# Attention transposed in halves, its sums taken from ones beside V and inverted on GpSimd

## The reference

```python
def one_block(qi):
    s = jnp.einsum('bqhgd,bshd->bhgqs', qi, k).astype(jnp.float32)
    p = jax.nn.softmax(s, axis=-1).astype(v.dtype)
    return jnp.einsum('bhgqs,bshd->bqhgd', p, v)
...
def conformer_conv(u, conv_dw, conv_b, ln_g, ln_b, w_o):
    a, gt = u[..., :CONV_W], u[..., CONV_W:]
    g = a * jax.nn.sigmoid(gt)
```

## Time and profile before

| | |
|---|---|
| median of three runs | 2191.34 us (2189.56 to 2195.04) |
| the profiled execution's own time | 2191.78 us |
| its span, first to last instruction | 2190.0 us |
| PE busy | 2124.9 us, 97% |
| PE weight loads busy | 1789.5 us, 82% |
| DVE busy | 1329.9 us, 61% |
| ACT busy | 804.8 us, 37% |
| GpSimd busy | 787.1 us, 36% |
| mean granted clock of TensorE | 0.986 |

### The profile page before, as it was taken

The page is one execution under the profiler, slowest core; times in us unless marked ns, Lnnn a source line. Parts: engine busy times, 40 slices in busy tenths (PEclk is TensorE's granted clock), DMA queues, the critical chain, the costliest instruction groups (busy, mean ns, idle before and its releaser), DMA issues.

```text
span 2190.0 us, 28107 instructions
## 1 busy us (share of the span) xinstructions
PE 2124.9 (97%) x11340; PEld 1789.5 (82%) x11340; DVE 1329.9 (61%) x1809; ACT 804.8 (37%) x1189; POOL 787.1 (36%) x366
## 2 busy tenths in 40 slices
PE   9999999999999999999999999899999999999997
PEld 7877888888888888888888887778777877888885
DVE  7369899855873688847616785989854362111113
ACT  5457411233224522222212356662244353222223
POOL 3310123232435433323323365004344475444442
PEclk8999999999999999999999999999999999999998
DMA  7100012132453234533323313002232423322321
GB/s 274 58 30 1 25 57 64 34 121 92 142 164 108 73 128 126 183 116 126 106 78 115 93 66 111 20 1 82 86 93 82 143 79 97 96 94 90 96 87 67
DMA packets 63200, 202.62 MB, mean 93 GB/s; under 512 B 7136, under 2 KB 8416, under 8 KB 63072
## 3 DMA queue, kind: packets, MB, share of 16 engines
q1 hardware_dynamic: 58608, 191.56, 27.0%
q10 hardware_dynamic: 4464, 9.28, 1.2%
HBM read 195.17 MB, written 5.64 MB: 92 GB/s over the span
## 4 chain that ended last, share of the span: by engine, by line
PE 80%; DVE 15%; ACT 3%; issue 1%; DMA 1%; POOL 1%; ACTq 0%; DVEq 0%; POOLq 0%
PE ps L560 73%; DVE conv_acc L1716 3%; DVE ps L1716 2%; DVE unit_stats L1677 2%; PE ps L586 1%; DVE pt1l L1697 1%; DVE pt0l L1697 1%; DVE probs L1691 1%; PE ps L795 1%; PE ps L629 1%; PE ps L647 1%; PE ps L638 1%; PE ps L816 1%; PE ps L668 1%; DMA w_raw<-in_w 1%
## 5 line engine op out<-in xcount | busy, mean ns | idle before, releaser
L455 POOL TENSOR_TENSOR w_l<-w_raw,w_h 128x1024 fp32r<-128x1024 f32 (+3 forms) x296 | 677.3, 2293 | 1283.0 <-ACT w_h L954 1282.9
L560 PE MATMUL ps<-h_h,w_h 128*128 128x512 f32 (+1 forms) x1296 | 428.0, 370 | 8.4 <-ACT t L1234 4.2
L560 PE MATMUL ps<-h_l,w_h 128*128 128x512 f32 (+1 forms) x1296 | 425.2, 368 | 0.0
L560 PE MATMUL ps<-h_h,w_l 128*128 128x512 f32 (+1 forms) x1296 | 424.7, 368 | 0.0
L954 ACT ACTIVATE w_h<-w_raw 128x1024 fp32r<-128x1024 f32 (+3 forms) x296 | 277.5, 939 | 236.0 <-PE ps L560 148.7
L560 PEld LDWEIGHTS ps<-h_h,w_h 128*128 128x128 f32 x1296 | 243.3, 188 | 59.0 <-ACT t L1234 6.0
L560 PEld LDWEIGHTS ps<-h_h,w_l 128*128 128x128 f32 x1296 | 244.4, 189 | 44.0
L560 PEld LDWEIGHTS ps<-h_l,w_h 128*128 128x128 f32 x1296 | 243.9, 188 | 42.6 <-issue 1.2
L1547 DVE CUSTOM_DVE_ANT_0 ps<-ada_raw,c_row 128x1024 f32<-128x1024 f32 x160 | 271.0, 1694 | 10.5 <-DMA ada_raw<-in_ada 5.4
L560 PE MATMUL ps<-f_h,w_h 128*128 128x258 f32 (+1 forms) x672 | 173.1, 339 | 0.9 <-DVE t L1902 0.9
L560 PE MATMUL ps<-f_h,w_l 128*128 128x258 f32 (+1 forms) x672 | 173.5, 340 | 0.0
(11 more groups left out here) (256 smaller groups left out, 3220.9 us busy)
## 6 DMA issues: line engine op xcount, KB each, us to landing
w_raw<-in_w SPq DMA_DIRECT2D x216, 512.0 KB, 3.6
ada_raw<-in_ada SPq DMA_DIRECT2D x80, 512.0 KB, 3.7
w_raw<-in_w SPq DMA_DIRECT2D x56, 256.0 KB, 3.2
w_raw<-in_w SPq DMA_DIRECT2D x16, 384.0 KB, 3.1
ada_near<-in_ada SPq DMA_DIRECT2D x10, 512.0 KB, 10.2
ada_far<-in_ada SPq DMA_DIRECT2D x6, 512.0 KB, 14.8
x_again<-in_x ACTq DMA_DIRECT2D x8, 384.0 KB, 7.5
x_between<-x SPq DMA_DIRECT2D x8, 384.0 KB, 2.9
```

The source lines that it names most:

```text
L455: nc.gpsimd.tensor_tensor(wl[:, s % RING, 0:n], raw[:, s % RAW, 0:n], wh[:, s % RING, 0:n], ALU.subtract).then_inc(split, 1)
L560: ins = nc.tensor.matmul(at(out, c0, c1), w[:, s % RING, b * P:(b + 1) * P], m[:, kt, first + c0:first + c1], start=(kt == 0 and n == 0), ...
```

## The change

- The exponential leaves the probabilities as they are: they are no longer summed on ACT nor multiplied on DVE. V's high part is kept once for each key-value head, as 64 columns of V beside 64 columns of ones. The value product with it gives the output on partitions 0 to 63 and, on partitions 64 to 127, the sum of the probabilities, 64 times over. Both are evicted, the sum into `ada_raw` (`o_sum`).
- For each pair of heads GpSimd then runs `divide_by_sums`: `pow(sum, -1)`, three instructions for one Newton step on it, and the multiplication of `o_raw`. Each waits for the one before it.
- Transposes, high parts and low parts come in halves of three (or two) blocks, and each half of B is a buffer of its own.
- The transposes of a unit wait for its exponential alone; the value products start one turn of the loop later.
- The scores of units 0 and 1 are issued inside the gemm of `cval` (after five and seven of its eight blocks), unit 0 into OD; their maxima and the first exponential move ahead in DVE's and ACT's programs.
- `o_high` and `o_low` of the last row block come later: behind the gate of the next convolution block on ACT, behind the first eleven taps on DVE. GpSimd's weight splits after the first of attention wait behind all four divisions.

```diff
+            def divide_by_sums(ly, lo, j):
+                last_b = max(b for h, _, _, _, _, b in units(ly) if h == 2 * j + 1)
+                pool.wait_ge(*seen("free", "pv", ly, last_b))
+                total, inverse = o_sum(j)[:, lo:T], (t1[:, lo:T] if j < BR - 1 else o_sum(j - 1)[:, lo:T])
+                chain(nc.gpsimd.tensor_tensor(inverse, total, minus_one[:, 0:1].to_broadcast([P, T - lo]), ALU.pow))
+                chain(nc.gpsimd.tensor_tensor(total, total, inverse, ALU.mult))
+                chain(nc.gpsimd.tensor_scalar(total, total, -1.0, 2.0, ALU.mult, ALU.add))
+                chain(nc.gpsimd.tensor_tensor(inverse, inverse, total, ALU.mult))
+                chain(nc.gpsimd.tensor_tensor(o_raw[:, j, lo:T], o_raw[:, j, lo:T], inverse, ALU.mult), "o", ly, j)
...
+                split_run(at_s, ly * SLABS + S_CONV + 1 + RING)
+                at_s = ly * SLABS + S_CONV + 1 + RING
+                pool.wait_ge(*seen("free", "cval", ly, 0))
+                for j in range(BR):
+                    divide_by_sums(ly, lo, j)
...
+                gemm(A[1], [(s0 + S_CONV + 1, 8)], hh, hl, cols, within={5: lambda: scores(0), 7: lambda: scores(1)})
...
-                        for n, (v, p) in enumerate(((vh, ph), (vh, pl), (vl, ph))):
-                            ins = nc.tensor.matmul(ODs[b % 2][0:HD, 0:2 * P], v[:, k, d0:d0 + HD], p[:, k, :],
-                                                   start=(k == 0 and n == 0), stop=(k == nk // P - 1 and n == 2))
+                        out = ODs[b % 2][:, 0:2 * P]
+                        nc.tensor.matmul(out, vh[h // 4][:, k, :], ph[:, k, :], start=(k == 0), stop=False)
+                        nc.tensor.matmul(out[0:HD], vl[:, k, d0:d0 + HD], ph[:, k, :], start=False, stop=False)
+                        ins = nc.tensor.matmul(out, vh[h // 4][:, k, :], pl[:, k, :], start=False,
+                                               stop=(k == nk // P - 1))
...
-                for u in range(len(us) + 2):
+                transposes(0)
+                for u in range(1, len(us) + 3):
                     if u + 1 < len(us):
                         scores(u + 1)
-                    if 1 <= u <= len(us):
-                        transposes(u - 1)
                     for step in plan.get(u, ()):
                         values(*step)
+                    if 2 <= u <= len(us):
+                        transposes(u - 1)
...
-                        link(v.reciprocal(ust[:, 3, c:c + n], ust[:, 2, c:c + n]), dve_tmp)
-                        for r in range(n):
-                            p_r = pr[:, (u - 1) % 2, r * nk:(r + 1) * nk]
-                            v.tensor_scalar(p_r, p_r, ust[:, 3, c + r:c + r + 1], None, ALU.mult).then_inc(
-                                *(dve_tmp.up("normed", ly, u - 1) if r == n - 1 else dve_tmp.up()))
```

More of the change, by code:

```diff
@@ L335, in value_steps @@
             todo, out = [], {}
[L336 to L340, removed]
+            for u in range(3, len(us) + 3):
+                if us[u - 3][3] == us[u - 3][4] - 1:
+                    parts = 1 if us[u - 3][2] == CTX else 2
+                    todo += [(u - 3, part, parts) for part in range(parts)]
+                n = 1 if u < len(us) + 2 else len(todo)
                 out[u], todo = todo[:n], todo[n:]
@@ L547, in take, with gemm @@
                 last_use[w] = name
-            def gemm(out, slabs, xh, xl, cols, k_ready=None, first=0):
+            def gemm(out, slabs, xh, xl, cols, k_ready=None, first=0, within={}):
                 kt = 0
@@ L773, in scores @@
                     h, q0, nk, q, nq, b = us[u]
-                    take(u % 2, "scores", ly, u)
+                    take("OD" if u == 0 else (u + 1) % 2, "scores", ly, u)
                     if u == 0:
@@ L1140, in _, with exponentials @@
                 q_high("q3")
+                us = units(ly)
+                def exponentials(u):
+                    h, q0, nk, q, nq, b = us[u]
+                    act.wait_ge(*seen("negmax", ly, u))
+                    if u >= 2:
+                        act.wait_ge(*seen("pt", ly, u - 2, 1))
+                    n, c = q_tiles(us[u]), 2 * (u % 8)
+                    for r in range(n):
+                        nc.scalar.activation(pr[:, u % 2, r * nk:(r + 1) * nk],
+                                             at(score_tile(u), r * nk, (r + 1) * nk), ACT.Exp,
+                                             bias=ust[:, 1, c + r:c + r + 1], scale=q_scale(us[u])[:, r:r + 1]).then_inc(
+                            *(act_out.up("free", "scores", ly, u) if r == n - 1 else act_out.up()))
+                exponentials(0)
                 result_of(s0 + S_CONV + 1)
-                us = units(ly)
                 act.wait_ge(*seen("tile", ly, "q3"))
@@ L1178, in _ @@
-                    for v, part, parts in plan.get(u - 1, ()):
+                        for half in range(2):
+                            act.wait_ge(*seen("pt", ly, u - 1, half))
+                            nc.scalar.activation(key_rows(pt(b)[0], us[u - 1], half), by_key(turned(us[u - 1], half)),
+                                                 ACT.Copy).then_inc(*act_hi.up("pth", ly, u - 1, half))
+                    for v, part, parts in plan.get(u, ()):
                         if part == parts - 1:
@@ L1701, in _, with o_low @@
-                for j in range(BR):
+                        for half in range(2):
+                            dve.wait_ge(*seen("pth", ly, u - 2, half))
+                            v.tensor_tensor(key_rows(pl, us[u - 2], half), by_key(turned(us[u - 2], half)),
+                                            key_rows(ph, us[u - 2], half), ALU.subtract).then_inc(
+                                *dve_lo.up("free", "pt", ly, u - 2, half))
+                def o_low(j):
                     dve.wait_ge(*seen("oh", ly, j))
@@ L1704, in _ @@
                         *dve_lo.up("ol", ly, j))
+                for j in range(BR - 1):
+                    o_low(j)
                 a0 = 0 if lo == 0 else GL - HALF
```

161 lines of the change are left out of this document (89 added, 72 removed).

## The result

The changed kernel takes 2880.93 us, the median of four runs (2879.45 to 2881.82), against 2190.45 us for the kernel before on the same chip: a ratio of 1.315 (95% interval 1.313 to 1.317), 690 us slower. The forecast was 2174 us, in a range to 2198. The profiled execution has a span of 2877.7 us.

A forecast was written before the change was run, and what follows sets the result against it. The prediction took DVE to bound attention in the second layer and a ring through DVE, PE and ACT in the first, with PE next. From 2191.8 us, 31 less for shorter attentions plus 13 for division gave 2174, range 2161 to 2198.

The forecast's parts named there:

- The price of the power: GpSimd's power in the division: taken at 10 ns a column, 7.7 us at 768 columns and 5.1 at 512.
- the last division: End of each attention: only this division meets the end; earlier ones hide, pairs coming every 23 us, 20 in layer two.
- rival of the dear power: GpSimd's division: each ns a column costs 1.28 us, break-even at 24, 2212 us at 40; chance 0.22.
- The loop: Both attentions: PE bounds at 2.48 us a unit, first-layer head 11.8 us; 17 and 14 us saved, 31 together.
- the rival of ACT and the waits: Attention loops: these bind instead of PE, 12.5 us a head and 2.65 a unit, 2183 us; chance 0.16.
- The costs of a cheap division: Behind the attentions: 6.5 us in the first layer, 5.6 in the second, 1 for splits, about 13 in all.
- power cheap: GpSimd's division: power under 4 ns a column, so the division costs 4 us and the time is 2165; chance 0.14.
- no lock: End of both attentions: DVE runs on during the power, last block's `o_l` ready in time, near 2163 us; no separate chance.
- The lock: End of attention: DVE instructions with two SBUF inputs wait out GpSimd's power; DVE late by power + 2 and power + 1.5.
- The copy of rows 9: Trace before the change: a 0.41 us copy took 2.57 beside a 2.40 us GpSimd split, read as DVE being held.
- the first `o_l` ends with the power: End of attention: sign expected if the prediction was right, DVE's first such low part held until GpSimd's power finishes.
- The tile: PE's value products: switching 128 and 64 stationary columns costs 0.08 us a change, 0.5 a unit, 2206 us; chance 0.05.

The follow-up runs named there:

- e6: Changed kernel with the power kept only for each layer's last pair of heads, a multiplication by -1 for the other three; 2357.96 us, ratio 1.077.
- e2: Changed kernel with each power over only 48 of 768 columns (32 of 512), output not divided rightly; 2166.19 us, ratio 0.990.
- e1: Changed kernel with every power replaced by a multiplication by -1 on GpSimd, output not divided; 2168.03 us, ratio 0.990.
- e9: Changed kernel, sums on ACT, inverses per unit on DVE, turned into rows by f32 matmuls on PE, one GpSimd multiplication; 2172.37 us, ratio 0.993.
- e10: e2 with the scores of units 0 and 1 put behind the gemm instead of inside it; 2173.08 us, ratio 0.992.
- e12: As e9, but GpSimd splits the inverses in two fp32r parts, which PE turns with fp32r products; 2171.25 us, ratio 0.992.
- e5: Changed kernel with the division on ACT: sums evicted as logarithms, one exponential with scale -1 per pair of heads; 2283.76 us, ratio 1.043.

## Why the prediction was wrong

**The price of the power** is the step that failed: taken at 10 ns a column with ends of 2.4 and 40, it measures 160. No row bore on it, and the upper end was not a bound from a row but a guess at what a series of arithmetic steps might cost. The text said that it fell with this number, yet left 0.14 above the range.

**Only the last division was priced.** "In the loop it is hidden: a pair of heads comes every 23 us" was true of the price taken and false of the real one. The prediction mentions that beyond that distance the division would hold up ACT, but neither it nor its rival of the dear power puts a time on that. The runs divide the loss: with the price measured, the prediction's own formula (1.28 us for each ns a column, for one power in each layer) gives 2191.8 - 31 + 205 = 2366, and e6, which has just that, took 2358. The other 523 us are the three earlier pairs, which queue on GpSimd in one row.

**The loop** was right but for size. Forecast 11.8 us a head and 2.48 us a unit; e2 has 12.35 and 2.53. The first layer's head is near where the rival of ACT and the waits put it (12.5), the second layer's unit near PE's own figure (2.48). The windows of e2 (start:end, length, then busy time of PE, weight loads, DVE, ACT and GpSimd) agree: in the second layer nothing but PE is near its limit, in the first PE's modelled busy time leaves 4 us and ACT is the next.

```profile
141.00:231.00 90.00, 85.83 (x656) 79.52 (x656) 68.61 (x142) 76.82 (x160) 43.12 (x15) 1.00 0.00 1
1376.00:1446.00 70.00, 69.13 (x519) 63.82 (x517) 52.30 (x103) 56.41 (x111) 31.22 (x16) 1.00 0.01 1
```

In time I count from the start of the gemm in front of each attention to the start of the one behind it. Before, the first took from 124.14 to 248.49, 124.4 us, and the second from 1370.07 to 1472.23, 102.2 us. In e2 they take from 121.20 to 231.66, 110.5 us, and from 1353.20 to 1443.54, 90.3 us. That is 13.9 us less where 17 was forecast and 11.8 where 14 was: 25.7 us of 31. The starts of the gemms in front in the chains, the second of before, then both of e2:

```profile
1370.07 5.59 PE ps L560 x24
```

```profile
121.20 5.27 PE ps L600 x30
...
1353.20 3.49 PE ps L600 x15
```

PE's first attention does end at 231.7, as forecast (231), but partly by luck: 2.9 us of it are an earlier start of the gemm in front. That is scatter between executions, for in e1, whose program is the same up to there, that gemm starts at 118.80.

**The costs of a cheap division** were too high. Between the end of the first attention and PE's start on the feed-forward part lie 499.9 us before and 499.7 in e2 (before, then e2):

```profile
L560 PE MATMUL ps<-f_h,w_h x672: 280/388/403, 748.4 to 1237.9; 128*128 128x258 f32 x168
```

```profile
L600 PE MATMUL ps<-f_h,w_h x672: 280/388/403, 731.4 to 1221.0; 128*128 128x258 f32 x168
```

So a power of 8 us costs the first layer nothing that can be seen, where the sum had 6.5 for one of 7.7. From the end of the second attention to the end of the span it is 717.8 us before and 719.3 in e2: 1.5 us instead of 5.6, and in other runs the same stretch is between 715.9 (e9) and 721.2 (e10), so this figure too lies within the scatter. Behind both terms stands the step that DVE stands still for the power. It doesn't, up to 512 columns. Whether a standing DVE would have cost that much stays open; in e1 GpSimd's ordinary operations hold DVE for some 4 us in the first layer (5.55 and 1.95 us instead of 2.70 and 0.63), and the time is that of e2. The two errors, some 5 us too much for the loops and some 11 too much for the division, are opposite: at the price that it took, the prediction would have come out 8 us too high (2174 against e2's 2166). The rival "power cheap" gave 2165 and "no lock" 2163; e2 took 2166.2, e1 2168.0.

**The lock.** The copy of rows 9 was read rightly: GpSimd's ordinary operations hold DVE (e1, and `o_l` of 1.84 us beside a split in e2). What failed is to carry that over to the power. Its sign, "the first `o_l` ends with the power", is not there in e2. The Trainium skill, "SBUF — State Buffer", section "Who interferes with whom", makes the shared pair of ports a lock for the whole instruction. For powers of 48, 384 and 512 columns the runs show none of it; for 768 they show it for a stretch as long as 512 columns take, or to the end. The measurement decides; why 768 differs is open, and since powers between 512 and 768 columns were not run, so is where it begins.

**The tile** did not cost anything. Value products of the changed kernel, whose stationary operand changes between 128 and 64 columns:

```profile
148.17 0.28 PE L862 MATMUL ps<-pt1h,v_first 128*128 128x256 f32 x1
148.29 0.28 PE L863 MATMUL ps<-pt1h,v_l 128*64 128x256 f32 x1
148.41 0.28 PE L864 MATMUL ps<-pt1l,v_first 128*128 128x256 f32 x1
```

They start 0.12 us apart, into the narrow tile and out of it, as the products of the kernel before do, so no drain of the rival's 0.08 us a change is there, and 2206 goes with it.

**What stays open.** e12 has loops within 0.5 us of e2's each and less work on GpSimd behind them, but is 5 us slower (0.9923 against 0.9899, with intervals that overlap). From its first scores to the gemm behind the first attention it takes 107.9 us where e2 takes 105.3 (123.56 to 231.42, 126.31 to 231.66), and another 4 us go between the attentions, a stretch that its edits don't touch. Since e1 too is 2.8 us longer there than e2, at least part of them is the scatter of single executions; how much wasn't tried.

## What to carry to other kernels

Before an operation that no trace has shown goes on the path, run it once by itself: one unknown price of 160 ns a column outweighed every other term by twenty to one, and its row would have ended the matter. Where an engine off the path gets a new job, compare the length of the job with the distance at which the jobs come; as soon as it is longer, the price is paid for each of them and not for the last alone. And in these runs a per-query sum was cheapest to invert where it is one column: invert it there (0.15 us) and let PE turn it, rather than invert a row spread over 64 partitions.

## What the runs showed of the hardware

- GpSimd's power costs 160 ns a column on 128 partitions, 67 times what its subtraction costs, with a fixed part of some 0.4 us at most (a line through 8.01 us for 48 columns and 122.64 for 768 also meets 61.52 for 384 and 81.91 for 512).
- It leaves DVE's operations with two SBUF inputs and its copies alone in instructions of 48, 384 and 512 columns, and holds them for 82 and 40 us in one instruction of 768 (82 and 38 in e6).
- GpSimd's multiplication by a column of a tile takes 2.21 us for 768 columns, by constants 0.83.
- ACT reloads its tables, 1.28 us, each time it goes from exponential to logarithm or back, 72 times in e5 as built here.
- Changing the stationary tile between 128 and 64 columns costs PE nothing that can be seen: 0.12 us from start to start, as without the change.
- An f32 product of 128 columns with a new stationary operand of 64 comes every 0.15 us. It leaves two rows of 0.27 us each in the trace, which overlap: a price is read from start to start.
